# A gather-bound expert stage: the first head's routing split in two halves of eight rows, with the dot operand's scaling between them

## The chip, the cores and the metric

The kernel runs on one core of one Trainium2 chip. The metric is the device time of one execution in microseconds. Below, TensorE is PE, VectorE is DVE, ScalarE is ACT, GpSimd is POOL and SyncE is SP, as in the profile.

## What is computed

Two transformer-like blocks follow each other over 256 tokens of width 1024. The change touches only the second half of the first block, a mixture of experts whose rows are looked up by two-part keys:

```python
def _peer(h, w_q, sub_keys_1, sub_keys_2, expert_u, expert_v):
    q = (h @ w_q).reshape(B, S, PEER_HEADS, PEER_DKEY)
    s1 = jnp.einsum('bshd,nd->bshn', q[..., :half], sub_keys_1)
    s2 = jnp.einsum('bshd,nd->bshn', q[..., half:], sub_keys_2)
    v1, i1 = lax.top_k(s1, PEER_TOPK)
    v2, i2 = lax.top_k(s2, PEER_TOPK)
    cand = (v1[..., :, None] + v2[..., None, :]).reshape(..., PEER_TOPK * PEER_TOPK)
    best, ci = lax.top_k(cand, PEER_TOPK)
    expert_idx = i1[ci // PEER_TOPK] * PEER_NKEYS + i2[ci % PEER_TOPK]
    gates = jax.nn.softmax(best, axis=-1)
    ...
    a = jax.nn.gelu(einsum('td,thkd->thk', hx, u)) * gx
    return einsum('thk,thkd->td', a, v)
```

There are 8 heads, 128 keys on each side, 16 rows chosen for each token and head, and `h` is the normed, scaled and shifted residual (`h2` in the code). A row of the table `experts` holds `u` and `v` of one expert, 2048 float32 numbers or 8 KB.

## The kernel before

All five engines run hand-written instruction streams that are tied together by semaphores; nothing reorders them. 256 tokens are two tiles of 128, so there are 16 "heads" of work: eight for the first tile of tokens, eight for the second.

**Queries and scores.** PE multiplies the residual by the query weights in 16 blocks, `query(b)` (lines 1114 to 1149 order them), each as three passes (lines 770 to 772: the high part of the operands with the high part, and each low part with the other's high part). The weights come in eight chunks, `pq` 0 to 7, two blocks each. For a chunk ACT writes the high part (`part`, line 1346, semaphore `w_hi`) and DVE the low part (`rest`, line 1959, semaphore `w_lo`), and PE waits for `w_lo` before the first product of a block. `head_scores(h)` multiplies two blocks by the keys; DVE's `scores(h, t)` scales the result into `s_all` and counts up the semaphore `scores`.

**The operand of the dots.** DVE scales the residual by the norm (line 2425, semaphore `n2_scaled`), ACT adds the shift (`shift_h2`, line 1599, semaphore `h2`), PE transposes it in four steps (`turn_h2(0..3)`, line 1080; the third waits for four counts of `scores`, because it writes into banks that the scores of head 1 were in), and ACT copies it to `h2tok` (line 1620).

**Routing.** For a head DVE picks the top 16 keys on each side, adds them into 256 candidates, picks the best 16 and turns them into row numbers `rowid`. `route(h, even)` does it in one go (lines 2321 to 2361, then `name_rows`, whose line 2304 counts up `rows_ready`). It is used for heads 0 and 1; later heads have the same work spread between their dots.

**Gathers, dots, values.** POOL's `first_rows` (lines 684 to 703) issues indirect DMAs (line 659), one for each row slot: 128 expert rows, 1 MB. It waits for `rows_ready` 1, issues slots 0, 1, 4, 5 of head 0; waits for `query(5)` and issues slots 2, 3, 6, 7; waits for `rows_ready` 2 and issues slots 0, 1 of head 1 (`pair(1, 1, 0)`, into the memory of head 0's slots 0, 1, so after their use), then slots 2, 3 of head 1 (`pair(1, 1, 1)`, which waits until `values(1)` has used head 0's slots 2, 3), then slots 8, 9 of head 0, and so on. The slots 0 to 7 share a home with the next head's, and all wait for `v_used`, which PE counts up. DVE's `dot` (line 2377) multiplies two slots with `h2tok`, ACT's `weigh` (lines 1604 to 1615) makes diagonal matrices of the results, and PE's `values(p)` (line 1109) adds the weighted second halves.

**The order on DVE around the change** is the code at lines 2418 to 2456: scores of head 0, `route(0, 0)`, the scaling, `both_scores(1)`, `rest()`, the softmax weights, the first pair of dots, `route(1, 1)`, the second pair. The `rest()` there makes the low part of chunk `pq` 4, which is for PE's `query(8)` and `query(9)`. Those stand on PE after `values(0)` and `head_scores(3)` and before `values(1)` and `values(2)`. On ACT, `soften(0)` (line 1562, the exponentials of head 0) waits for the semaphore `best` and stands ahead of `shift_h2`.

Of the kernel before, what the change touches and what calls it, by code (L numbers as in the profile page):

```python
# [17 lines left out]
ALU = mybir.AluOpType  # L18
ACT = mybir.ActivationFunctionType
X = mybir.AxisListType.X  # L20

P = 128
# [3 lines left out]
KD = D // P  # L26
# [12 lines left out]
TAKEN = -3e38  # L39
# [183 lines left out]
def two_blocks(nc, w, out):  # L223
    with ExitStack() as ctx:
# [1078 lines left out]
        def _(act):  # L1303
# [254 lines left out]
            def soften(g):  # L1558

                act.wait_ge(S("best"), g + 1)  # L1560
                act.sem_inc(S("tick"), 1)
                act.activation(expb, best, ACT.Exp, bias=gst[:, 0:1], accum_out=gst[:, 1:2]).then_inc(S("best_exp"), 1)
# [19 lines left out]
            def copy_shifted(h):  # L1582


                act.wait_ge(S("score_mm"), 2 * h + 1)
                if h >= 2:
                    act.wait_ge(S("scores"), NT * (h - 1))
                at = h % 2 * 2 * NKEY
                act.activation(shifted[:, at:at + 2 * NKEY], BK[3][:, at:at + 2 * NKEY], ACT.Copy).then_inc(S("shifted"), 1)
# [3 lines left out]
            act.wait_ge(S("norm_ss"), norm_count("n2"))  # L1593
            inverse_root(stat[:, 1, :], BK[5][:, 0:T], D, "n2_root")

            def shift_h2():
                for k in range(KD):
                    act.wait_ge(S("n2_scaled"), k + 1)
                    act.activation(hT[:, k, :], hT[:, k, :], ACT.Identity, bias=adaT[:, 24 + k:25 + k]).then_inc(S("h2"), 1)

# [31 lines left out]
            part()  # L1632
            take_query(4)
            copy_shifted(1)
            soften(0)
            shift_h2()
            take_query(5)
            for i in range(4):
                copy_h2(i)
# [267 lines left out]
        def _(v):  # L1907
# [398 lines left out]
            def route(h, even):  # L2306
# [54 lines left out]
                v.sem_inc(S("head_step"), -n[0])  # L2361
                name_rows(even)

            def soft_weights(g, even):

                v.wait_ge(S("best_exp"), g + 1)
                v.sem_inc(S("tick"), 1)

                def body(step):
                    step(v.reciprocal(gst[:, 2:3], gst[:, 1:2]))  # L2370
                    step(v.tensor_scalar(soft[:, even, :], expb, gst[:, 2:3], None, ALU.mult))
                by(body)
# [45 lines left out]
            v.wait_ge(S("n2_root"), 1)  # L2418
            link(v.reciprocal(csil[:, 0:2], csil[:, 2:4]))
            scores(0, 0)  # L2420
            route(0, 0)
            scores(0, 1)
            v.wait_ge(S("n2_root"), 2)
            for k in range(KD):
                stt(hT[:, k, :], xT[:, k, :], mod[:, k:k + 1], stat[:, 1, :]).then_inc(S("n2_scaled"), 1)
            both_scores(1)
            rest()
            soft_weights(0, 0)
            v.wait_ge(S("h2tok"), 2)
            dot(0, 0, 0, 0)  # L2430
            route(1, 1)
            dot(0, 0, 0, 1)
            both_scores(2)
            dot(0, 0, 0, 2)
# [420 lines left out]
```

## Time and profile before

| | us |
|---|---|
| median of 3 runs | 1351.63 (1350.41 to 1352.51) |
| the profiled execution's own time | 1353.7 |
| its span | 1352.0 |
| PE busy | 1215.2 (90%) |
| DVE busy | 1059.7 (78%) |
| ACT busy | 616.0 (46%) |
| POOL busy | 290.1 (21%) |
| DMA of the gathers (queue 0) | 268.45 MB of 416.64 MB |

The page gives busy time for each engine, a picture of the span in 40 slices of 33.8 us (the digits are tenths of busy time; GB/s is what the DMA engines moved), and groups of instructions. Busy PE isn't PE at its peak, and the share of the whole span says little here: the stage of the change runs from about 307 us to 360 us, and the gathers behind it go on to about 950 us. So the rows below are read from the timeline and from stretches of it.

### The profile page before, as it was taken

The numbers are of one execution on the slowest core, as the hardware profiler recorded it, in microseconds if no ns is written. First come the engines' busy times: TensorE is split into PE (matmuls) and PEld (weight loads), VectorE is DVE, ScalarE is ACT, GpSimd is POOL, SyncE is SP. The second block draws the span as 40 slices with busy tenths as digits, with TensorE's granted clock in tenths as the row PEclk, the third lists the DMA queues.
The fourth block names the chain that finished last, engine by engine and source line by source line (L and its number), as shares of the span: only waits on it lengthen the run. The fifth ranks groups of instructions, "written<-read, shape, count | busy, mean of one in ns | idle before, by whom it ended". The sixth has DMA issues, their size and how long they took to land. (4 is left out here: it accounts for less than half of the span.)

```text
span 1352.0 us, 19494 instructions
## 1 busy us (share of the span) xinstructions
PE 1215.2 (90%) x6952; PEld 908.0 (67%) x6952; DVE 1059.7 (78%) x2161; ACT 616.0 (46%) x1265; POOL 290.1 (21%) x280
## 2 busy tenths in 40 slices
PE   7999999999989877778877777787899999999998
PEld 5999999999743333324332232333699999999998
DVE  7898678887879777777766777777699978898666
ACT  4666555656333333332433333233563265554445
POOL 1010000002545544344444434443000000000000
PEclk9999999999999999999999999999999999999999
DMA  9966446665999999999999999999853545454461
GB/s 388 384 225 249 187 158 235 245 234 234 375 422 426 427 428 428 427 427 427 427 427 427 427 428 428 428 427 428 341 187 126 187 137 183 180 187 173 174 236 43
DMA packets 55488, 416.64 MB, mean 308 GB/s; under 512 B 6113, under 2 KB 6753, under 8 KB 9202
## 3 DMA queue, kind: packets, MB, share of 16 engines
q0 software_dynamic: 37152, 268.45, 47.2%
q1 hardware_dynamic: 17792, 146.51, 29.3%
q8 instruction: 50, 0.82, 0.2%
q10 hardware_dynamic: 466, 0.63, 0.1%
q14 instruction: 28, 0.23, 0.0%
HBM read 414.52 MB, written 1.05 MB: 307 GB/s over the span
## 5 line engine op out<-in xcount | busy, mean ns | idle before, releaser
L1109 PE MATMUL ps<-arena 128*128 128x512 f32 x512 | 234.6, 603 | 57.0 <-ACT arena L1613 57.0
L1109 PE MATMUL ps<-ring,arena 128*128 128x512 f32 x440 | 214.1, 637 | 47.1 <-ACT arena L1613 47.1
L2377 DVE CUSTOM_DVE_ANT_0 arena<-arena 128x1024 f32<-128x1024 f32 x128 | 151.7, 1223 | 99.0 <-DMA arena<-in_experts,rowid 96.3
L1109 PEld LDWEIGHTS ps<-arena 128*128 128x128 f32 x512 | 92.7, 189 | 193.9 <-ACT arena L1613 98.0
L659 POOL DMA_INDIRECT arena<-in_experts,rowid x128 | 128.7, 1005 | 351.7 <-DVE rowid L2304 191.0
L1109 PEld LDWEIGHTS ps<-ring,arena 128*128 128x128 f32 x440 | 86.1, 202 | 170.4 <-issue 92.6
L772 PE MATMUL ps<-h_hi,w_lo 128*128 128x256 f32 x700 | 194.9, 278 | 0.0
L1606 ACT ACTIVATE arena<-arena 128x2 f32<-128x2 f32 x126 | 25.6, 203 | 369.1 <-DVE arena L2377 368.9
L770 PE MATMUL ps<-h_hi,w_hi 128*128 128x256 f32 x672 | 189.0, 281 | 3.0 <-DVE w_lo L1959 2.4
L771 PE MATMUL ps<-h_lo,w_hi 128*128 128x256 f32 x672 | 187.2, 279 | 0.0
L2377 DVE CUSTOM_DVE_ANT_0 ring<-ring,arena 128x1024 f32<-128x1024 f32 x112 | 133.3, 1222 | 35.4 <-DMA ring<-in_experts,rowid 26.5
L659 POOL DMA_INDIRECT ring<-in_experts,rowid x110 | 127.1, 1155 | 133.2 <-PE ps L1109 98.9
L1959 DVE TENSOR_TENSOR w_lo<-arena,w_hi 128x4096 fp32r<-128x4096 f32 (+1 forms) x30 | 122.1, 4069 | 29.7 <-ACT w_hi L1346 29.1
L1346 ACT ACTIVATE w_hi<-arena 128x4096 fp32r<-128x4096 f32 (+1 forms) x30 | 100.4, 3346 | 76.2 <-DMA arena<-in_up_w 32.1
L772 PEld LDWEIGHTS ps<-h_hi,w_lo 128*128 128x128 f32 x700 | 132.3, 189 | 0.0
L770 PEld LDWEIGHTS ps<-h_hi,w_hi 128*128 128x128 f32 x672 | 127.3, 190 | 4.1 <-DVE w_lo L1959 3.0
L771 PEld LDWEIGHTS ps<-h_lo,w_hi 128*128 128x128 f32 x672 | 127.1, 189 | 0.2
L770 PE MATMUL ps<-n_hi,e_hi 128*128 128x256 f32 (+1 forms) x352 | 101.4, 288 | 0.2 <-issue 0.2
L771 PE MATMUL ps<-n_lo,e_hi 128*128 128x256 f32 (+1 forms) x352 | 98.1, 279 | 0.0
L772 PE MATMUL ps<-n_hi,e_lo 128*128 128x256 f32 (+1 forms) x352 | 98.1, 279 | 0.0
L1959 DVE TENSOR_TENSOR e_lo<-ring,e_hi 128x2048 fp32r<-128x2048 f32 (+1 forms) x38 | 86.3, 2271 | 11.4 <-ACT e_hi L1346 10.8
L1613 ACT ACTIVATE arena<-ident,arena 128x128 f32<-128x128 f32 x252 | 85.4, 386 | 0.0
(424 smaller groups left out, 2558.4 us busy)
## 6 DMA issues: line engine op xcount, KB each, us to landing
ring<-in_early_w SPq DMA_DIRECT2D x43, 1024.0 KB, 5.0
arena<-in_ada_w SPq DMA_DIRECT2D x24, 1024.0 KB, 8.1
arena<-in_up_w SPq DMA_DIRECT2D x11, 2048.0 KB, 7.8
arena<-in_z_w SPq DMA_DIRECT2D x8, 2048.0 KB, 7.9
arena<-in_down_w SPq DMA_DIRECT2D x8, 1408.0 KB, 6.1
arena<-in_o_w SPq DMA_DIRECT2D x2, 2048.0 KB, 8.1
arena<-in_early_w SPq DMA_DIRECT2D x3, 1024.0 KB, 7.6
arena<-in_experts,rowid POOLq DMA_INDIRECT x128
```

The lines of the kernel that those rows point to most:

```text
L659: pool.indirect_dma_start(out=rows[j], out_offset=None, in_=w["experts"], in_offset=bass.IndirectOffsetOnAxis(ap=rowid[:, even, j:j + 1], ...
L770: pe.matmul(out, hi[:, k, c0:c0 + m], x_hi[:, k, :], start=k == 0, stop=False, skip_group_check=True)
L771: pe.matmul(out, hi[:, k, c0:c0 + m], x_lo[:, k, :], start=False, stop=False, skip_group_check=True)
L772: return pe.matmul(out, lo[:, k, c0:c0 + m], x_hi[:, k, :], start=False, stop=k == KD - 1, skip_group_check=True)
L1109: mm = pe.matmul(BK[4 + 2 * t + b], diag[:, j, :], rows[j][:, D + b * 512:D + (b + 1) * 512], start=first and j == 0, stop=last and j == ( ...
L1346: act.activation(hi, whole, ACT.Copy).then_inc(S("w_hi"), 1)
L1606: act.activation(gel[:, even, two], dots[:, even, two], ACT.Gelu).then_inc(S("act_head"), 1)
L1613: act.activation(diag[:, j, :], ident[:, :], ACT.Copy, scale=amul[:, even, j:j + 1]).then_inc(S("diag"), 1)
L1959: v.tensor_tensor(lo, whole, hi.bitcast(F32), ALU.subtract).then_inc(S("w_lo"), 1)
L2377: v.tensor_tensor_reduce(out=u, in0=u, in1=h2tok[:, t, :], scale=1.0, scalar=0.0, op0=ALU.mult, op1=ALU.add, accum_out=dots[:, even, j:j + ...
```

## The change

The first head's routing, `route(0, 0)`, becomes three pieces. `route_first` does the top keys of both sides, the candidates and the best eight with their positions. `name_eight(slice(0, 8))` turns these eight into row numbers and counts up `rows_ready`. After the scores of the second tile and the scaling of the dot operand, `route_second` picks the other eight (and counts up `best`), and `name_eight(slice(8, 16))` names them. The `rest()` for chunk `pq` 4 goes from ahead of the softmax weights to behind `route(1, 1)`. On ACT, `shift_h2` is cut in two: four of its eight instructions now stand ahead of `soften(0)`. `soft_weights` here is unchanged.

```diff
@@ ACT
-            def shift_h2():
-                for k in range(KD):
+            def shift_h2(ks):
+                for k in ks:
...
             take_query(4)
             copy_shifted(1)
+            shift_h2(range(4))
             soften(0)
-            shift_h2()
+            shift_h2(range(4, KD))
             take_query(5)
@@ DVE
+            def route_first():
...
+                for i in range(2):
+                    found = mark(v.max_index(topu[:, i, 8:16], top[:, i, 8:16], more[i]))
+                after(sums)
+                high = mark(v.max(best[:, 0:8], cand.rearrange("p a b -> p (a b)")))
+                after(found)
+                v.tensor_copy(topi[:, :, :], topu[:, :, :])
+                after(high)
+                after(mark(v.max_index(ciu[:, 0, 0:8], best[:, 0:8], cand.rearrange("p a b -> p (a b)"))))
+                v.sem_inc(S("head_step"), -n[0])
+
+            def name_eight(js):
...
+                def body(step):
+                    v.tensor_scalar(ciu[:, 1, js], ciu[:, 0, js], 4, None, ALU.logical_shift_right)
+                    step(v.tensor_scalar(ciu[:, 2, js], ciu[:, 0, js], EK - 1, None, ALU.bitwise_and))
+                    step(v.tensor_copy(ci[:, :, js], ciu[:, 1:3, js]))
+                    step(v.tensor_tensor(
+                        found, iota16[:, :].rearrange("p (c b a) -> p c b a", c=1, b=1).broadcast_to([P, 2, 8, EK]),
+                        ci[:, :, js].rearrange("p c (a b) -> p c a b", b=1).broadcast_to([P, 2, 8, EK]), ALU.is_equal))
+                    step(v.tensor_tensor(
+                        found, found, topi[:, :, :].rearrange("p c (b a) -> p c b a", b=1).broadcast_to([P, 2, 8, EK]),
+                        ALU.mult))
+                    step(v.tensor_reduce(pick[:, :, js], found, X, ALU.add))
+                    step(stt(pick[:, 0, js], pick[:, 0, js], float(NKEY), pick[:, 1, js], ALU.mult, ALU.add))
+                by(body)
+                return v.tensor_copy(rowid[:, 0, js], pick[:, 0, js])
+
+            def route_second():
...
+                def body(step):
+                    step(v.match_replace(cf2, best[:, 0:8], cf, TAKEN))
+                    step(v.max(best[:, 8:16], cf2))
+                    v.tensor_scalar(gst[:, 0:1], best[:, 0:1], -1.0, None, ALU.mult).then_inc(S("best"), 1)
+                    step(v.max_index(ciu[:, 0, 8:16], best[:, 8:16], cf2))
+                by(body)
...
             scores(0, 0)
-            route(0, 0)
+            route_first()
+            name_eight(slice(0, 8)).then_inc(S("rows_ready"), 1)
             scores(0, 1)
             v.wait_ge(S("n2_root"), 2)
             for k in range(KD):
                 stt(hT[:, k, :], xT[:, k, :], mod[:, k:k + 1], stat[:, 1, :]).then_inc(S("n2_scaled"), 1)
+            route_second()
+            name_eight(slice(8, EK))
             both_scores(1)
-            rest()
             soft_weights(0, 0)
             v.wait_ge(S("h2tok"), 2)
             dot(0, 0, 0, 0)
             route(1, 1)
+            rest()
             dot(0, 0, 0, 1)
```

On DVE, the first head from its ninth to sixteenth best on. Before, from the search for the second eight to the scaling:

```order
L2350 MAX_INDEX ciu<-arena 128x8
L2351 TENSOR_SCALAR ciu<-ciu 128x16
L2352 TENSOR_SCALAR ciu<-ciu 128x16
L2353 CAST arena<-ciu 128x32
L2354 TENSOR_TENSOR arena<-iota,arena 128x512
L2357 TENSOR_TENSOR arena<-arena 128x512
L2360 TENSOR_REDUCE arena<-arena 128x32
L1917 SCALAR_TENSOR_TENSOR arena<-arena 128x16
L2304 CAST rowid<-arena 128x16
L1917 SCALAR_TENSOR_TENSOR arena<-ps,csil,arena 128x256
L1917 SCALAR_TENSOR_TENSOR h_rows<-xT,mod,stat 128x256 x8
```

The same place on DVE in the changed kernel, from the search for the first eight's positions on:

```order
L2401 MAX_INDEX ciu<-arena 128x8
L2409 TENSOR_SCALAR ciu<-ciu 128x8
L2410 TENSOR_SCALAR ciu<-ciu 128x8
L2411 CAST arena<-ciu 128x2x8
L2412 TENSOR_TENSOR arena<-iota,arena 128x256
L2415 TENSOR_TENSOR arena<-arena 128x256
L2418 TENSOR_REDUCE arena<-arena 128x2x8
L1918 SCALAR_TENSOR_TENSOR arena<-arena 128x8
L2421 CAST rowid<-arena 128x8
L1918 SCALAR_TENSOR_TENSOR arena<-ps,csil,arena 128x256
L1918 SCALAR_TENSOR_TENSOR h_rows<-xT,mod,stat 128x256 x8
L2428 MATCH_REPLACE arena<-arena 128x256
```

The three wide instructions that name the rows have half the elements, and the second eight is picked only after the scaling; its naming repeats rows L2409 to L2421 once more, and only then come the scores of head 1.

On DVE, around the routing of head 1, whose last instruction writes `rowid`. Before, from its last wide instruction to the scores of head 2:

```order
L2360 TENSOR_REDUCE arena<-arena 128x32
L1917 SCALAR_TENSOR_TENSOR arena<-arena 128x16
L2304 CAST rowid<-arena 128x16
L2377 ISA arena<-arena 128x1024
L2377 ISA arena 128x1
L1917 SCALAR_TENSOR_TENSOR arena<-ps,csil,arena 128x256 x2
```

After:

```order
L2361 TENSOR_REDUCE arena<-arena 128x32
L1918 SCALAR_TENSOR_TENSOR arena<-arena 128x16
L2305 CAST rowid<-arena 128x16
L1960 TENSOR_TENSOR pq_ring<-ring,pq_ring 128x2048
L2447 ISA arena<-arena 128x1024
L2447 ISA arena 128x1
L1918 SCALAR_TENSOR_TENSOR arena<-ps,csil,arena 128x256 x2
```

The low part of chunk `pq` 4 now stands between the routing of head 1 and the second pair of dots (a pair is two such ISA instructions with a read of the sum behind each). On PE and POOL no instruction moves.

## Rows read from the trace of the kernel before

**Rows 1.** The page, part 2: what the DMA engines moved, in 40 slices.
```profile
GB/s 388 384 225 249 187 158 235 245 234 234 375 422 426 427 428 428 427 427 427 427 427 427 427 428 428 428 427 428 341 187 126 187 137 183 180 187 173 174 236 43
```

**Rows 2.** Stretches: length, engines' busy time (instructions), PEclk, DMA share, GB/s.
```profile
308.00:316.00 8.00, 8.00 (x66) 7.90 (x66) 7.79 (x34) 6.54 (x8) 0.00 (x0) 1.00 0.00 0
320.00:344.00 24.00, 23.32 (x166) 20.23 (x165) 19.36 (x55) 12.34 (x29) 8.52 (x8) 1.00 1.01 423
344.00:350.00 6.00, 6.00 (x20) 2.96 (x19) 5.75 (x10) 3.07 (x6) 2.70 (x3) 1.00 0.73 264
350.00:360.00 10.00, 10.00 (x66) 8.09 (x65) 9.22 (x24) 5.00 (x11) 7.89 (x5) 1.00 0.98 351
360.00:940.00 580.00, 466.17 (x1115) 199.02 (x1114) 432.83 (x1116) 200.42 (x670) 256.38 (x242) 0.97 1.01 427
```

**Rows 3.** Timeline of POOL: start, length, operation, idle before and its releaser.
```profile
316.99 1.09 POOL L659 DMA_INDIRECT arena<-in_experts,rowid  x1 [181.67 <-DVE rowid L2304]
...
323.12 1.37 POOL L659 DMA_INDIRECT arena<-in_experts,rowid  x1 [1.03 <-PE ps L772]
...
338.12 0.94 POOL L659 DMA_INDIRECT arena<-in_experts,rowid  x1 [9.29 <-DVE rowid L2304]
...
346.69 0.94 POOL L659 DMA_INDIRECT arena<-in_experts,rowid  x1 [6.33 <-PE ps L1109]
...
349.90 3.05 POOL L659 DMA_INDIRECT h_rows<-in_experts,rowid  x1 [0.30 <-issue]
...
357.87 2.97 POOL L659 DMA_INDIRECT arena<-in_experts,rowid  x1 [1.19 <-issue]
```

**Rows 4.** Timeline of PE around turn_h2, query(6), head_scores(3), query(8), values(1).
```profile
321.89 1.91 PE L1080 MATMUL ps<-ident,h_rows 128*128 128x128 f32 x16
323.55 0.36 PE L770 MATMUL ps<-x_hi,pq_ring 128*128 128x258 f32 x1
...
334.24 0.61 PE L1066 MATMUL ps<-keyT,arena 128*128 128x128 f32 x4
...
335.50 0.36 PE L770 MATMUL ps<-x_hi,pq_ring 128*128 128x258 f32 x1
...
342.18 0.70 PE L1109 MATMUL ps<-arena 128*128 128x512 f32 x1 [0.68 <-ACT arena L1613]
```

**Rows 5.** Timeline of DVE: routing of head 0, rest, dots, routing of head 1.
```profile
312.11 0.42 DVE L2345 FIND_INDEX8 ciu<-arena 128x8 uint32<-128x256 f32 x1
...
312.97 0.42 DVE L2350 FIND_INDEX8 ciu<-arena 128x8 uint32<-128x256 f32 x1
...
313.92 0.69 DVE L2354 TENSOR_TENSOR arena<-iota,arena 128x512 f32<-128x512 f32 x1
...
316.53 0.17 DVE L2304 CAST rowid<-arena 128x16 uint32<-128x16 f32 x1
...
321.38 2.29 DVE L1959 TENSOR_TENSOR pq_ring<-ring,pq_ring 128x2048 fp32r<-128x2048 f32 x1
...
326.79 1.23 DVE L2377 CUSTOM_DVE_ANT_0 arena<-arena 128x1024 f32<-128x1024 f32 x1 [2.77 <-DMA arena<-in_experts,rowid]
...
337.11 0.17 DVE L2304 CAST rowid<-arena 128x16 uint32<-128x16 f32 x1
```

**Rows 6.** Timeline of DVE, later: the same naming steps on 256 elements.
```profile
380.92 0.42 DVE L2295 TENSOR_TENSOR arena<-arena 128x256 f32<-128x256 f32 x1
381.38 0.42 DVE L2298 TENSOR_REDUCE arena<-arena 128x16 f32<-128x256 f32 x1
```

**Rows 7.** Timeline of DVE: two later low parts, beside two gathers of rows 3.
```profile
349.85 2.28 DVE L1959 TENSOR_TENSOR pq_ring<-ring,pq_ring 128x2048 fp32r<-128x2048 f32 x1
...
357.74 2.29 DVE L1959 TENSOR_TENSOR pq_ring<-ring,pq_ring 128x2048 fp32r<-128x2048 f32 x1
```

**Rows 8.** Timeline of ACT: the shifts of the dot operand; the last diagonals before values(1).
```profile
318.87 3.31 ACT L1599 ACTIVATE h_rows<-h_rows,adaT 128x256 f32<-128x256 f32 x8
...
341.45 0.68 ACT L1613 ACTIVATE arena<-ident,arena 128x128 f32<-128x128 f32 x2
```

More of the change, by code:

```diff
@@ L2362, in route, with mark, after @@
                 name_rows(even)
+            def route_first():
+                n = [0]
+                def mark(ins):
+                    n[0] += 1
+                    ins.then_inc(S("head_step"), 1)
+                    return n[0]
+                def after(at):
+                    v.wait_ge(S("head_step"), at)
+                keys = [s_all[:, 0, i * NKEY:(i + 1) * NKEY] for i in range(2)]
+                more = [cur2[:, i * NKEY:(i + 1) * NKEY] for i in range(2)]
+                first = [mark(v.max(top[:, i, 0:8], keys[i])) for i in range(2)]
+                left = []
+                for i in range(2):
+                    after(first[i])
+                    left.append(mark(v.match_replace(more[i], top[:, i, 0:8], keys[i], TAKEN)))
+                second = []
+                for i in range(2):
+                    after(left[i])
+                    second.append(mark(v.max(top[:, i, 8:16], more[i])))
+                for i in range(2):
+                    v.max_index(topu[:, i, 0:8], top[:, i, 0:8], keys[i])
+                after(second[1])
+                sums = mark(v.tensor_tensor(cand, top[:, 0, :].rearrange("p (a b) -> p a b", b=1).broadcast_to([P, EK, EK]),
+                                            top[:, 1, :].rearrange("p (b a) -> p b a", b=1).broadcast_to([P, EK, EK]),
+                                            ALU.add))
+                for i in range(2):
+                    found = mark(v.max_index(topu[:, i, 8:16], top[:, i, 8:16], more[i]))
[6 more added lines that the diff above has]
+                v.sem_inc(S("head_step"), -n[0])
@@ new lines, in name_eight @@
+            def name_eight(js):
+                found = oneh.rearrange("p a b -> p (a b)").rearrange("p (c a b) -> p c a b", c=2, b=EK)
+                def body(step):
[12 more added lines that the diff above has]
+                return v.tensor_copy(rowid[:, 0, js], pick[:, 0, js])
@@ new lines, in route_second @@
+            def route_second():
+                cf, cf2 = cand.rearrange("p a b -> p (a b)"), cand2.rearrange("p a b -> p (a b)")
+                def body(step):
[4 more added lines that the diff above has]
+                by(body)
```

## The prediction

> **What bounds the kernel now.** I read the 40 slices first. From about 372 us to 946 us the DMA engines move 422 to 428 GB/s in every slice [rows 1]: that is the ceiling this kernel reaches, so the long middle of the kernel is bound by the gathers' bytes. Then I cut the part ahead of it into stretches [rows 2]. From 308 to 316 us nothing is moved; from 320 to 344 us the engines are full (423 GB/s); from 344 to 360 us they are not (264, then 351 GB/s); from 360 to 940 us they are full again at 427 GB/s. So the time at which the gathers end is the time at which the last hole closes, near 360 us, plus bytes that the change doesn't alter. Lost in the hole, against 427 GB/s: 6 x (1 - 264/427) + 10 x (1 - 351/427) = 2.3 + 1.8 = 4.1 us. An earlier first gather is worth something only if this hole doesn't grow by as much.
>
> What opens the hole is on POOL's timeline [rows 3]: after the pair at 338.12 us POOL stands idle for 6.33 us until PE (line 1109, values(1)) releases it at 346.69 us. And PE isn't waiting for gathers there: it is busy for 23.3 of the 24 us from 320 to 344 us [rows 2], with one gap of 0.68 us ahead of values(1) at 342.18 us, which ended with the diagonals that ACT began at 341.45 us [rows 4, 8]. So the hole is closed by PE's chain turn_h2, query(6), query(7), values(0), head_scores(3), query(8), query(9), values(1), then POOL's issues.
>
> **The earlier start.** Before, the first eight's positions are found by 312.11 + 0.42 = 312.53 us with a replace of 0.5 us ahead of that search, the wide steps take 0.69 us each, and rowid is written by 316.53 + 0.17 = 316.70 us [rows 5]. The new chain leaves out the replace (about 0.4 us), the second max and the second search (0.86 us: from 312.53 us to that search's end at 312.97 + 0.42 = 313.39 us [rows 5]), and runs three wide steps at 0.42 instead of 0.69 us [rows 5, 6], 0.81 us together. That is 0.4 + 0.86 + 0.81 = 2.07 us, and I take 2.05 us: rowid's first eight at 314.65 us, POOL's first issue at 314.94 instead of 316.99 us. POOL's next four wait for query(5) at 323.12 us [rows 3], the same as before, since PE is untouched up to there. The first four gathers are 4.2 MB, 9.8 us at 427 GB/s, so the engines stay fed until then.
>
> **The later second half, on DVE.** What was left out comes back after the scaling: replace, max and search (0.4 + 0.86 us and the waits between them, about 1.5 us) and a second naming (313.39 to 316.70 us before, 3.3 us, less the 0.81 us: about 2.45 us). The scaling itself starts 2.05 us earlier. So head 1's scores end at 321.34 - 2.05 + 1.5 + 2.45 = 323.2 us instead of just before 321.38 us [rows 5]: 1.9 us late. PE's third turn_h2 waits for them. The 16 transposes run from 321.89 to 323.55 us, so the third group is due at 321.89 + 8 x 0.104 = 322.7 us [rows 4]. PE stalls for about 0.6 us, and query(6) starts at 324.15 us. The halved shift on ACT costs nothing: eight shifts take 3.31 us from 318.87 us [rows 8]; four now go first, soften(0) (its `best` counts up near 319.4 us) takes its place at about 320.3 us, and the last shift ends near 322.2 us as before.
>
> **The moved low part.** This is the costly edit. The first pair of dots waited for its rows at 326.79 us [rows 5]; with the gathers 2.05 us earlier it starts at 324.75 us (DVE is free at 323.7 us, h2tok is there near 324.3 us). Dots and route(1, 1) take 10.5 us as before (326.79 to 337.28 us [rows 5]), so head 1's rows are named at 335.25 instead of 337.28 us. Only then comes the low part of chunk pq 4, 2.29 us [rows 5]: ready at 337.5 us, where it used to be ready at 323.67 us. query(8) needs it. PE started query(8) at 335.50 us [rows 4] and, with the 0.6 us above, would be there at 336.1 us. So it stalls for another 1.4 us and starts 2.0 us late. Before values(1) 0.68 us of that, and the time for the weights' load, is given back, because PE was waiting there: query(8) and query(9) took 5.85 us, so values(1) starts at 337.5 + 5.85 = 343.35 instead of 342.18 us [rows 4]. Its diagonals are no later: the second pair of dots ends near 339.9 us, ACT takes query(8) at 340.7 us and has the diagonals by 342.4 us. So POOL is released at 346.69 + 1.17 = 347.86 us [rows 3].
>
> **The sum.** The gathers' queue, 2.05 us ahead, now also runs dry 2.05 us earlier (near 344.7 us), and that gain is spent in the hole. What counts is how much later the hole closes: at most the 1.17 us of PE's chain. Part of that is returned by POOL itself. Its two longest issues, 3.05 us at 349.90 us and 2.97 us at 357.87 us (0.94 us is usual) [rows 3], stand beside DVE's low parts at 349.85 and 357.74 us [rows 7], and both end 0.8 us after them. The low part of 349.85 us comes about 0.75 us earlier now, since DVE leads there; that of 357.74 us comes 0.35 us later, as the scores of head 4 must come from PE first (due at 354.75 instead of 354.41 us). So the issue that is released at 357.87 + 1.17 = 359.04 us should end at 361.2 instead of 360.84 us: 0.35 us late. Between 0.35 and 1.17 us, I take 0.8 us. The rest of the kernel behind the gathers is shifted, not changed. Against the profiled execution: 1353.7 + 0.8 = 1354.5 us. That execution lies 2.1 us above the median of the runs, so the forecast for the median is 1351.63 + 0.8 = 1352.4 us.
>
> On these long issues the Trainium skill, "SBUF — State Buffer", section "Who interferes with whom", says that a VectorE instruction with two inputs in SBUF keeps GpSimd from reading through a port that both share, and that the one that comes second waits for all of the first. By that, moving a two-input low part to 335.2 us puts it on top of POOL's issues for head 1 (due at 336.07 us) and holds the first of them to about 338.3 us, so that this pair gains nothing over its 338.12 us. The rows 3 and 7 agree with the rule (3.05 us beside 2.28 us). It would not change the sum, if the queue still holds work until 339.8 us, but it takes the reserve away; the rival with the larger hole below is what it leads to if it doesn't.
>
> **Rivals.** (a) *The gain comes through.* If the hole is not set by PE's release but by how much has been gathered before, the whole earlier start counts: 1351.63 - 2.05 = 1349.6 us. For it: between 350 and 360 us the engines are busy (0.98) while moving only 351 GB/s [rows 2], so something other than a missing issue slows them there. Against it: POOL's idle 6.33 us before 346.69 us [rows 3], with a queue that ends just then. Chance 0.17. (b) *The hole grows on both sides and slows the rest, slower than before.* The queue is dry from 344.7 us until the issue of 347.86 us takes effect. If the DMA engines come back slower from an empty queue than from one nearly empty, or if values(3), 1.17 us late, opens a second hole before 359.04 us, the hole costs another 1 to 2.5 us: 1351.63 + 1.2 + 1 to 2.5 = 1353.8 to 1355.3 us. It decides as soon as what is queued at 347.86 us and behind doesn't last until 360 us. Chance 0.15. (c) *PE's stall doesn't happen as computed*, since the first dots start earlier than the landing suggests or query(8) meets its low part in time; then start and hole cancel: 1351.6 us. Chance 0.13. (d) Something larger in either direction, 0.05 faster and 0.02 slower.
>
> **Numbers.** The forecast (1352.0 to 1352.8 us) has 0.48. Within 0.2%, which is 2.7 us and about what a measurement of this kernel can tell from no change, lie the forecast, (a), (c) and nearly two thirds of (b): together 0.87, rounded down. Faster by more than 0.2% 0.06, slower by more 0.07. The range takes in (a) with 0.3 us for the spread of the runs, and (b) up to 1354.3 us.
>
> **What would show it.** In the profile after: first gather near 314.9 us; head 1's scores ending near 323.2 us, and a gap of about 0.6 us in PE's transposes; rowid of head 1 near 335.2 us, the low part right behind it, and a PE gap of about 1.4 us ahead of query(8) at 337.5 us; no gap before values(1) at 343.4 us; POOL's release near 347.9 us; fewer GB/s from 344 to 350 us than 264. If PE shows no gap ahead of query(8), the argument is wrong; if the gaps are there and the time still falls by 2 us, the reading of the hole is.

## The result and the profile after

| | kernel before | changed kernel |
|---|---|---|
| median, first measurement (22 runs each) | 1351.60 us | 1354.15 us |
| lowest to highest | 1349.58 to 1356.58 | 1351.72 to 1363.47 |
| ratio, 95% interval | | 1.0034 (1.0022 to 1.0046) |
| the profiled execution's own time, its span | 1353.7, 1352.0 | 1352.29, 1350.6 |

The changed kernel is slower, where no measurable difference was forecast: the measured ratio is 1.0034, as is that of the means, while that of the medians is 1.0019 (2.55 us). The means lie further apart because 8 of the 22 executions of the changed kernel took over 1359 us and none of the kernel before did; without executions above 1356.4 us the medians are 1353.62 and 1351.57 us, 2.05 us apart. Two later measurements of the same pair, on other chips, gave 1.0016 (0.9998 to 1.0035) and 1.0016 (0.9999 to 1.0033), which by themselves don't exclude "no change". The profiled execution is one of the shorter ones of the changed kernel, and that of the kernel before one of its longer ones, so their spans alone would say the opposite. Both kernels have some executions about 6 us longer than the others; what is different in these is shown under e8.

First the stage that the prediction was about. These are the stretches of [rows 2] in the changed kernel:

```profile
320.00:344.00 24.00, 22.66 (x164) 19.91 (x164) 22.02 (x63) 12.60 (x32) 8.79 (x7) 1.00 1.01 417
344.00:350.00 6.00, 6.00 (x16) 2.66 (x14) 5.75 (x8) 3.90 (x10) 2.07 (x2) 1.00 0.19 82
350.00:360.00 10.00, 10.00 (x64) 8.00 (x63) 7.99 (x24) 3.96 (x7) 6.86 (x6) 1.00 0.96 369
360.00:940.00 580.00, 464.02 (x1122) 198.87 (x1121) 433.02 (x1116) 200.65 (x670) 255.04 (x242) 0.98 1.01 427
```

From 344 to 350 us only 82 GB/s are left of 264; behind it the rate is a little higher (369 instead of 351), and from 360 us on it is the same 427. Lost against 427 GB/s: 6 x (1 - 82/427) + 10 x (1 - 369/427) = 4.8 + 1.4 = 6.2 us, 2.1 us more than before. The gathers start 1.98 us earlier. So gain and loss cancel, as the prediction had it in kind. POOL's timeline, for [rows 3]:

```profile
315.01 1.09 POOL L659 DMA_INDIRECT arena<-in_experts,rowid  x1 [179.51 <-DVE rowid L2421]
...
335.93 2.17 POOL L659 DMA_INDIRECT arena<-in_experts,rowid  x1 [8.06 <-DVE rowid L2305]
338.40 1.98 POOL L659 DMA_INDIRECT arena<-in_experts,rowid  x1 [0.31 <-issue]
347.63 1.98 POOL L659 DMA_INDIRECT arena<-in_experts,rowid  x1 [7.24 <-PE ps L1109]
...
358.72 2.21 POOL L659 DMA_INDIRECT arena<-in_experts,rowid  x1 [1.93 <-PE ps L1109]
```

PE's, for [rows 4]; the gaps stand in brackets with what ended them:

```profile
323.38 1.09 PE L1080 MATMUL ps<-ident,h_rows 128*128 128x128 f32 x8 [0.37 <-DVE arena L1918]
324.23 0.37 PE L770 MATMUL ps<-x_hi,pq_ring 128*128 128x258 f32 x1
...
337.34 0.39 PE L770 MATMUL ps<-x_hi,pq_ring 128*128 128x258 f32 x1 [0.97 <-DVE pq_ring L1960]
...
343.22 1.02 PE L1109 MATMUL ps<-arena 128*128 128x512 f32 x2
```

and DVE's, for [rows 5]:

```profile
324.59 1.22 DVE L2447 CUSTOM_DVE_ANT_0 arena<-arena 128x1024 f32<-128x1024 f32 x1 [0.66 <-DMA arena<-in_experts,rowid]
...
334.92 0.17 DVE L2305 CAST rowid<-arena 128x16 uint32<-128x16 f32 x1
335.00 2.29 DVE L1960 TENSOR_TENSOR pq_ring<-ring,pq_ring 128x2048 fp32r<-128x2048 f32 x1
```

Every local step came within 0.5 us of its forecast. What the prediction had not looked at is the end of the gathers. Here is DVE over the last pairs of dots, kernel before:

```profile
948.08 1.23 DVE L2377 CUSTOM_DVE_ANT_0 h_rows<-h_rows,arena 128x1024 f32<-128x1024 f32 x1 [1.99 <-DMA ring<-in_experts,rowid]
...
953.01 1.23 DVE L2377 CUSTOM_DVE_ANT_0 ring<-ring,arena 128x1024 f32<-128x1024 f32 x1 [2.54 <-DMA ring<-in_experts,rowid]
...
957.90 1.23 DVE L2377 CUSTOM_DVE_ANT_0 ring<-ring,arena 128x1024 f32<-128x1024 f32 x1 [2.51 <-DMA ring<-in_experts,rowid]
```

and changed kernel:

```profile
947.73 1.23 DVE L2447 CUSTOM_DVE_ANT_0 h_rows<-h_rows,arena 128x1024 f32<-128x1024 f32 x1 [2.00 <-DMA ring<-in_experts,rowid]
...
953.61 1.22 DVE L2447 CUSTOM_DVE_ANT_0 ring<-ring,arena 128x1024 f32<-128x1024 f32 x1 [3.50 <-DMA ring<-in_experts,rowid]
...
958.51 1.23 DVE L2447 CUSTOM_DVE_ANT_0 ring<-ring,arena 128x1024 f32<-128x1024 f32 x1 [2.52 <-DMA ring<-in_experts,rowid]
```

At 947.7 us the changed kernel is 0.35 us ahead. Its next pair waits 3.50 us for rows instead of 2.54 us, and from there on it is 0.6 us behind. (Below, this is the late pair: 5.88 us behind the pair ahead of it instead of 4.93 us.) In the DMA records an instruction packet of 8192 bytes (queue 14) starts at 951.5 us in the changed kernel; in the kernel before it starts at 961.5 us, when the last rows are in. The change puts ten DVE instructions more into the program (nine of them in the trace, and a semaphore wait), so everything behind them stands ten places further on, and the fetch comes ten places earlier. Whether that is the cause is what the second round of experiments asked.

### The profile page after: what moved, and what is told of

It is laid out like the page before. It is cut to its first block and busy times, and to the rows that moved or that the text cites. A ratio compares the mean times of both kernels' runs of the same rounds, so it can differ in the third digit from the quotient of the medians.

```text
span 1350.6 us, 19503 instructions
## 1 busy us (share of the span) xinstructions
PE 1211.1 (90%) x6952; PEld 906.0 (67%) x6952; DVE 1060.8 (79%) x2169; ACT 616.8 (46%) x1265; POOL 289.0 (21%) x280
## 3 DMA queue, kind: packets, MB, share of 16 engines
HBM read 414.52 MB, written 1.05 MB: 308 GB/s over the span
## 5 line engine op out<-in xcount | busy, mean ns | idle before, releaser
L1109 PE MATMUL ps<-ring,arena 128*128 128x512 f32 x440 | 211.0, 629 | 50.1 <-ACT arena L1613 50.1
```

The lines of the kernel that those rows point to most:

```text
L1109: mm = pe.matmul(BK[4 + 2 * t + b], diag[:, j, :], rows[j][:, D + b * 512:D + (b + 1) * 512], start=first and j == 0, stop=last and j == ( ...
```

## Experiments

Each ran on one chip beside runs of the kernel before. Single executions reach the change's stage at up to 2.1 us different times (first search of the first head's routing at 308.14 to 310.21 us), so for comparisons I subtract that time: "T+" is measured from the first MAX8 of this routing (308.50 us in the kernel before, 308.60 us in the changed one). On that clock the 251st gather's first packet starts at T+635.33 before, and the pair of dots that starts at 957.90 us before is at T+649.40.

### Which part of the change costs what

**e1, the changed kernel again,** with no edit.

> The changed kernel as it is, once more, to see how its single runs lie. The 22 runs so far fall into two groups: 12 near 1353.4 us (before: 1351.6), two near 1355.9, eight from 1359.3 to 1363.5. Theory (two parts): the hole in the gathers' queue closes about 1 to 2 us later in every run, and in about one run of three something adds another 7 to 8 us; so again two groups, with the same places, also on this one chip. Rival (chips differ, not runs): all runs here lie in one group, within 2 us of each other.

Measured 1354.31 us, ratio 1.0016 (0.9998 to 1.0035). One of the 11 executions lay near 1360 us, not one in three; in the kernel before, on the same chip, 5 of 28 took more than 1357 us. So the long executions aren't the changed kernel's own. Gathers at T+635.13. The late pair is there again, at 953.24 us, 5.88 us behind the one ahead of it. And in this execution there was a dip of PE's granted clock from 957.8 us on. PE over the last weighted sums, kernel before, then e1:

```profile
956.86 7.13 PE L1109 MATMUL ps<-ring,arena 128*128 128x512 f32 x16 [1.22 <-ACT arena L1613]
```

```profile
957.09 8.83 PE L1109 MATMUL ps<-ring,arena 128*128 128x512 f32 x16 [2.18 <-ACT arena L1613]
```

The same 16 matmuls take 1.70 us more, and the gap ahead of them is 0.96 us longer. The stretch from 957 to 962 us shows the clock (the eighth value: busy times, then PEclk, DMA share, GB/s), before and e1:

```profile
957.00:962.00 5.00, 5.00 (x12) 2.24 (x13) 4.10 (x7) 2.29 (x8) 0.00 (x0) 1.00 0.47 160
```

```profile
957.00:962.00 5.00, 4.91 (x8) 2.13 (x9) 3.86 (x7) 2.11 (x9) 0.00 (x0) 0.66 0.40 147
```

A mean of 0.66 over 5 us is 3.4 us at half (1.2 GHz) and the rest at full clock (2.4 GHz), and 1.7 us of work are lost. They aren't made up later: e6 and e10 are one program, the first with such a dip at 956.3 us and the second with none behind 950 us, and they end at T+1043.05 and T+1041.25.

**e2, the low part back at its old place,** the rest of the change kept.

```diff
             both_scores(1)
+            rest()
             soft_weights(0, 0)
...
             route(1, 1)
-            rest()
             dot(0, 0, 0, 1)
```

> The changed kernel with the low part of chunk pq 4 back ahead of the softmax weights. Theory (PE's stall ahead of query(8) makes the hole, and the dry queue is what the slow runs start from): no gap ahead of query(8), first dots at about 326.0 us instead of 324.6, rows of head 1 named near 336.5 us, POOL released at 346.8 to 347.0 us instead of 347.6, median 1351.6 us (1351.0 to 1352.3) and no runs near 1360 us. Rival (the split of the routing itself, by its earlier gathers, puts the queue into the slow group): runs near 1360 us are as frequent as in the changed kernel, median above 1353 us.

Measured 1352.54 us, ratio 1.0001 (0.9986 to 1.0017), 1.8 us below e1 on the same chip. PE has no gap ahead of query(8), POOL is released earlier, and the hole is smaller:

```profile
346.15 0.94 POOL L659 DMA_INDIRECT arena<-in_experts,rowid  x1 [5.92 <-PE ps L1109]
```

```profile
344.00:350.00 6.00, 6.00 (x24) 3.37 (x23) 5.75 (x8) 3.34 (x7) 3.24 (x3) 1.00 0.62 208
```

208 GB/s from 344 to 350 us instead of 82; gathers at T+633.97, 1.2 to 1.5 us ahead of the changed kernel. So the moved low part is what turns the earlier start into nothing. The late pair of dots is still there (5.89 us). The expected end of the long executions didn't come: two of 12 took 1357.9 and 1358.4 us, so that the dry queue isn't what makes them.

**e3, the low part moved alone,** in the kernel before (`rest()` behind `route(1, 1)`, nothing split).

> The kernel before with only the low part of chunk pq 4 moved behind route(1, 1). Theory (PE's chain closes the hole): the low part is ready near 339.5 us, query(8) starts 4.0 us late, of which 0.7 to 0.9 us is given back ahead of values(1), POOL is released near 349.8 us instead of 346.7, median 1351.6 + 3.1 = 1354.7 us or more, and many runs near 1361 us if a dry queue starts the slow group. Rival (the hole is not set by PE): within 0.5 us of 1351.6 us.

Measured 1357.71 us, ratio 1.0058 (1.0041 to 1.0074). Without the earlier start the low part comes later still, and POOL is released 4.5 us later than before on the T+ clock (5.1 us by the rows):

```profile
351.82 2.70 POOL L659 DMA_INDIRECT arena<-in_experts,rowid  x1 [8.73 <-PE ps L1109]
```

```profile
350.00:360.00 10.00, 10.00 (x51) 6.89 (x50) 6.80 (x18) 4.83 (x12) 6.65 (x6) 1.00 0.47 160
```

Gathers at T+640.16, 4.8 us later. The cost of this edit therefore depends on the split: it is 4.8 us alone, and 1.8 us beside it (by the averages given in the last part). The last dots come at their usual pace here (4.90 us), and this kernel has no added instruction.

**e4, head 1's scores ahead of the second half,** on top of e2, to take away PE's stall in the transposes.

```diff
+            both_scores(1)
             route_second()
             name_eight(slice(8, EK))
-            both_scores(1)
             rest()
```

> As the kernel with the low part back, and head 1's scores ahead of the second half of head 0's routing, so that PE's transposes don't wait either. Theory (PE's stalls are all that costs): no gap in the transposes, PE as in the kernel before, POOL released at 346.7 us or up to 0.1 us earlier, median 1350.9 to 1351.6 us, no runs near 1360 us. Rival (the early first gathers are worth their 2.05 us once PE doesn't stall): 1349.6 us. Second rival (the early gathers bring the slow runs): some runs near 1360 us here too.

Measured 1354.76 us, ratio 1.0027 (1.0012 to 1.0043). The stall doesn't go but grows, with another releaser: PE now waits 1.05 us for ACT's shifts, since `soften(0)`, which waits for `best`, stands ahead of the second four of them.

```profile
323.68 1.53 PE L1080 MATMUL ps<-ident,h_rows 128*128 128x128 f32 x12 [1.05 <-ACT h_rows L1599]
```

Gathers at T+634.80; late pair and clock dip near 958 us both there. The theory expected 1350.9 to 1351.6 us and failed. The 0.37 us of stall were not worth an edit.

### The late pair: the fetch or the routing

**e5, the kernel before again,** with no edit, as a measure of the scatter.

> The kernel before, nothing changed, as a second profile and as a measure of how far two measurements of the same program lie apart. Theory 1 (what stands behind 945 us decides): the ratio is 1.000 within 0.0015, the start of the last gathers lies within 1 us of the first profile's 943.8 us, and where the span differs by more than 1 us from 1352.0 us, the difference arises behind 945 us, as a dip of the granted clock near 958 us (about 1.7 us) or a slower pace of the matmuls between 1160 and 1320 us (about 6 us). Rival: the gathers' stage itself varies by 2 us or more between executions, and the last gathers start as far apart as the spans.

Measured 1350.52 us beside 1350.91 us, ratio 0.9990 (0.9975 to 1.0005), gathers at T+635.47. So a ratio 0.001 away from 1 is what one program can show against itself. Its trace joins the first one's up to 1150 us and then ends 1.9 us earlier: the first had a clock dip at 1160.7 us and this one none.

**e6, the kernel before with ten DVE instructions more,** ahead of the loop over heads (near 390 us, where DVE waits for rows anyway); the routing is untouched.

```diff
             name_rows(0)
+            for _ in range(5):
+                v.sem_inc(S("head_step"), 1)
+                v.sem_inc(S("head_step"), -1)
             with v.Fori(1, EH - 1, 2) as g:
```

> The kernel before with ten semaphore additions on DVE (five times plus one, minus one) ahead of the first loop over heads, where DVE has slack. Nothing of the routing is changed, but DVE's later instructions stand ten places further on, as they do in the changed kernel. Theory 1 (the fetch of DVE's instructions): the 8192-byte packet of the instruction queue moves from 961.5 us to about 951.5 us, the sixth pair of dots of the last head comes 5.9 us behind the fifth instead of 4.9 us (near 954 us), and the time is 1 us above that of the kernel before (ratio 1.0007). Rival: the later sixth pair belongs to the changed routing, and here the interval stays at 4.9 us and the time at that of the kernel before, wherever the packet lies.

Measured 1352.66 us beside 1350.91 us, ratio 1.0010 (0.9998 to 1.0022). The instruction packet moved to 949.8 us, and the late pair is there:

```profile
946.33 1.23 DVE L2377 CUSTOM_DVE_ANT_0 h_rows<-h_rows,arena 128x1024 f32<-128x1024 f32 x1 [1.99 <-DMA ring<-in_experts,rowid]
...
952.21 1.23 DVE L2377 CUSTOM_DVE_ANT_0 ring<-ring,arena 128x1024 f32<-128x1024 f32 x1 [3.51 <-DMA ring<-in_experts,rowid]
```

5.88 us instead of 4.93 us, with the routing of the kernel before. A clock dip near 957 us came with it.

**e7, the changed kernel with sixty such instructions** (thirty ahead of each loop over heads), which move the fetch to among the gathers.

> The changed kernel with sixty semaphore additions on DVE, thirty ahead of each of the two loops over heads, so that the instruction packet of 951.5 us is fetched some 40 us earlier, among the gathers. Theory 1 (the fetch): the sixth pair of dots comes 4.9 us behind the fifth, as in the kernel before, and the time is 1 us below that of the changed kernel: 1353.3 us, ratio about 1.001 against the kernel before. Rival: the interval stays at 5.9 us. Should the additions (1 to 2 us at each place) hold up the dots of a head, the last gathers start up to 2 us later than 944.1 us, which neither of them forecasts.

Measured 1352.28 us, ratio 1.0014 (1.0000 to 1.0029). No packet between 936 and 968 us, and the pair is on time, with the changed routing:

```profile
947.82 1.23 DVE L2447 CUSTOM_DVE_ANT_0 h_rows<-h_rows,arena 128x1024 f32<-128x1024 f32 x1 [2.00 <-DMA ring<-in_experts,rowid]
...
952.74 1.23 DVE L2447 CUSTOM_DVE_ANT_0 ring<-ring,arena 128x1024 f32<-128x1024 f32 x1 [2.54 <-DMA ring<-in_experts,rowid]
```

So the late pair goes with the fetch and not with the routing: shown in both directions. The packets' records show how. The instruction packet takes 0.31 us, as long as one expert row, but the row packet that starts as it ends (951.83 us in the changed kernel) takes 0.84 us instead of 0.31 us. This is so in all seven traces with the fetch near 950 us, and in the others no row packet from 945 to 962 us takes over 0.4 us. The two make 0.84 of the 0.96 us. Among the gathers, from 400 to 945 us, a row packet of 0.5 to 0.85 us follows on every 8 KB instruction packet too (8 or 9 in each trace); there the rate from 360 to 940 us stays 427 GB/s. Why that row packet is long is not shown. Against the start of the 251st gather the pair behind the late one (957.90 us before) comes only 0.5 us later: 14.6 us behind it on average in the seven traces with the fetch near 950 us (14.44 to 14.99), 14.1 us in eight without (13.72 to 14.37; e12, with PE in another order, is left out). The rest of the 0.96 us is a lead that DVE had at 947 us and lost.

The Trainium skill, "Runtime: NRT & Kernel Launch", section "Instruction fetch mechanics", says that the sequencer fetches the next block through its own DMA queue while it executes the present one, and that crossing a block is mostly hidden. For DVE itself the traces agree: what ended its 3.50 us of waiting was the landing of rows. What isn't hidden is the effect on a transfer beside it, the row packet of 0.84 us.

**e8, both repairs:** e2's edit and the sixty instructions.

> The split routing with the low part of chunk pq 4 back at its old place, and the same sixty semaphore additions. With the low part back, the last gathers started at 942.3 us, 1.5 us ahead of the kernel before. Theory 1 (the start is worth 1.5 us and the fetch takes 1 us of it): sixth pair 4.9 us behind the fifth, time 1.5 us below the kernel before, 1350.1 us, ratio 0.9989. Rival (the gain of the gathers' stage is given back behind 960 us, by the phase of the clock dips or the pace of the late matmuls): the last gathers start near 942.3 us and the ratio is still 1.000 or above.

Measured 1350.57 us beside 1350.91 us, ratio 0.9996 (0.9983 to 1.0009); gathers at T+633.58, pair on time. The profiled execution, though, took 1358.25 us, and its trace shows where such an execution loses 6 us. The stretch from 1200 to 1260 us, dense query and feed-forward matmuls, kernel before and e8:

```profile
1200.00:1260.00 60.00, 60.00 (x532) 60.00 (x531) 54.34 (x82) 28.99 (x28) 0.00 (x0) 1.00 0.45 163
```

```profile
1200.00:1260.00 60.00, 60.00 (x512) 60.00 (x511) 52.62 (x81) 27.96 (x27) 0.00 (x0) 1.00 0.45 163
```

512 matmuls instead of 532 in the same 60 us, with a granted clock of 1.00 in both. Their starts are 117.9 ns apart instead of 113.0 ns, from about 1160 to 1330 us, while DVE's and ACT's instructions there last as long as ever (the same median within 0.01 us in every group). In the other traces the 117.9 ns appear as well, but only in stretches of 10 to 60 us, between 970 and 1150 us and near 1330 us. The long stretch was there in e2, e7 and e8 and in no other trace; e14 is the program of e7 and e11 that of e8, so it isn't the program's. The executions of 1359 to 1363 us in the first measurement are longer than these three, and none of them was traced.

### The same questions a second time

**e9, the kernel before with the sixty instructions.**

> The kernel before with sixty semaphore additions on DVE (thirty ahead of each loop, 2.8 us at each place by the 0.093 us that one took in the trace of the kernel with ten), so that its instruction packet is fetched among the gathers, not in the tail. Theory 1 (sixty additions cost nothing, as the gathers bound that stretch): last gathers start between 942.6 and 943.9 us as in three profiles of the routing before, sixth pair of dots 4.9 us behind the fifth, ratio 1.000. Then the ratio of the changed kernel with the same additions, 1.0014, is the cost of the changed routing without the fetch. Rival: the additions cost something themselves, and the ratio lies at 1.0005 to 1.001; then the changed routing is that much cheaper than 1.0014 says.

1351.40 us beside 1350.96 us, ratio 1.0007 (0.9999 to 1.0016); gathers at T+634.93, pair on time (4.92 us).

**e10, e6 again.**

> The same kernel as the first one with ten additions: a second profile and a second measurement of what the fetch at 950 us costs in all. Theory 1 (the fetch leaves PE idle ahead of 958 us, and that brings the clock dip near 958 us in many executions): sixth pair 5.9 us behind the fifth again, ratio 1.0007 to 1.0014 (1 to 1.9 us) against the kernel before, and with sixty additions in place of ten the ratio falls back to 1.000. Rival: the 1.75 us of the first measurement were chance, and ten and sixty additions give the same ratio.

1353.21 us, ratio 1.0017 (0.9998 to 1.0037): late pair (5.88 us), this time without a dip at 958 us. The medians with ten instructions thus lie 1.8 and 2.3 us above those beside them, with sixty 0.4 us. None of these intervals excludes 1.0000 by itself, so a cost of the fetch in time is likely but not shown.

**e11, e8 again.**

> The split routing with the low part at its old place and sixty additions, as run once before at a ratio of 0.9996. Theory 1 (the last gathers, 1.1 us ahead of the mean of three profiles of the routing before, are worth that much): ratio 0.9992, and in a profile without the slow matmuls of 1160 to 1320 us the span is 1.1 us below that of the kernel before. Rival (what is won at the gathers is lost again in the PE-bound tail): last gathers near 942.3 us again and a ratio of 0.9996 to 1.0005.

1351.58 us, ratio 1.0010 (0.9994 to 1.0027), gathers at T+633.18. Two measurements, 0.9996 and 1.0010: the 1.2 us by which its gathers lead don't show in the time, and no version that beats the kernel before was found. Nor was its theory (0.9992) met. On the T+ clock this execution ends at 1040.6 us, the kernels with the old routing and no dip behind 950 us (e5, e9, e10) at 1041.6, 1041.3 and 1041.3 us; that is a gain below what these measurements can hold.

**e12, the hole attacked directly:** on top of e8, PE's values(1) goes ahead of query(9), and ACT's diagonals for it ahead of taking query(8).

```diff
             query(8)
-            query(9)
             values(1)
+            query(9)
             values(2)
```

> The kernel of the run ahead of this with one more change: PE's values(1) stands between query(8) and query(9) instead of behind both, and ACT's diagonals for it ahead of taking query(8). This goes at the hole itself. Theory 1 (the hole is closed by PE's chain): the diagonals are there near 340.5 us, PE stands idle 1.3 us ahead of values(1), POOL is released near 344.8 instead of 346.2 us, but query(9) and all of PE behind it come 1.3 us later, so that a later release becomes late: last gathers within 0.7 us of 942.3 us, ratio 0.9996. Rival: bytes moved early count fully, the last gathers start 1.4 us earlier at 940.9 us, ratio 0.9986, which would beat both kernels. Third: PE's later releases decide, last gathers at 943.6 us, ratio 1.0003.

1356.68 us, ratio 1.0051 (1.0035 to 1.0067): all three theories were wrong. PE, from values(1) on:

```profile
341.24 5.40 PE L1109 MATMUL ps<-arena 128*128 128x512 f32 x8 [1.77 <-ACT arena L1613]
...
351.25 3.70 PE L1109 MATMUL ps<-arena 128*128 128x512 f32 x8 [1.73 <-ACT arena L1613]
```

PE starts values(1) 0.85 us earlier than e8, but the idle 1.77 us ahead of it is followed by a clock dip at 341.7 us, and the eight matmuls take 5.40 us where the next eight take 3.70 us. POOL is released at 347.44 us, later than in e2, and stands idle once more for 5.48 us ahead of its issue at 363.43 us. Gathers at T+638.02, 4.4 us later than e8. Moving a wait to where PE is otherwise busy cost the wait and the clock here; the idle 1.73 us ahead of 351.25 us, though, had no dip behind it.

### The changed kernel a third time

**e13, the changed kernel, and e14, it with the sixty instructions,** on one chip.

> The changed kernel as it is, a third time. Theory 1 (executions 6 us longer come by chance, at about one in six, in both kernels): 1 to 4 of some 12 executions above 1357 us, much as in the kernel before, the rest around 1352.5 to 1353.5 us, ratio 1.0015 to 1.0025; in the profile the last gathers start 635.3 us behind the first routing instruction of the first head and the sixth pair of dots 5.9 us behind the fifth. Rival (the change makes the slow pace frequent): 4 or more of 12, with 2 or fewer in 25 of the kernel before.

> The changed kernel with sixty semaphore additions, a second time. Theory 1: no fetch in the last dots, sixth pair 4.9 us behind the fifth, no clock dip near 958 us, ratio 1.0010 to 1.0015, and 1 to 1.5 us below the changed kernel without additions on the same chip. Rival: the two lie within 0.5 us of each other, and the fetch was not worth more than the 0.4 us by which the last dots come late.

e13: 1354.21 us, ratio 1.0016 (0.9999 to 1.0033); gathers at T+635.52, late pair (5.88 us), clock dip at 958.8 us. e14: 1353.19 us, ratio 1.0000 (0.9980 to 1.0019); gathers at T+635.60, pair on time (4.92 us), no dip. The median without the fetch is 1.0 us lower here, as expected, though the two intervals overlap. As to the long executions: above 1356.4 us lay 8 of 22 of the changed kernel and 1 of 22 of the kernel before in the first measurement, 2 of 11 and 5 of 28 in the second, 3 of 12 and 7 of 23 here. Together that is 13 of 45 and 13 of 73; on the two other chips the kernel before had 2 of 35 and 4 of 29. So the share differs from chip to chip, and the bound isn't sharp: e13's trace, at 1356.49 us, has two dips and no long slow stretch. That the change makes the slow matmuls more frequent is neither shown nor excluded.

**The dips.** In ten traces the granted clock dipped at 799 to 803 us and again 78.5 us later, at 877 to 881 us; one such step further is 956 to 960 us. Five of them have the fetch near 950 us, and four of these dipped near 958 us (e1, e4, e6, e13; not e10). Five don't have it (before, e8, e9, e11, e14), and none dipped there. This fits a dip that needs both the pattern, which differs from execution to execution, and the longer idle time of PE ahead of its last weighted sums (2.18 us in e1, 1.22 us before). The changed kernel's first trace and e2, whose pattern was another, had the fetch and no dip. Four of five against none of five is a hint and no proof; I didn't vary the idle time by itself.

## Why the prediction was wrong

- **The earlier start** (first issue 314.94 us, 2.05 us earlier): 315.01 us, right.
- **The later second half** (scores end 323.2 us, stall 0.6 us, query(6) 324.15 us): scores end at 323.3 us, stall 0.37 us, query(6) 324.23 us. Right.
- **The moved low part** (rowid of head 1 by 335.25 us, gap 1.4 us, query(8) 337.5 us): 335.1 us, 0.97 us, 337.34 us. The gap reads smaller since it counts from the modelled end of the last scores' matmul; from head_scores(3) to query(8) it took 337.34 - 334.87 = 2.47 us instead of 1.26 us [rows 4], so the delay is 1.2 us. Right, and e2, e8 and e11 show its worth: without it the gathers start at T+633.58 on average, 1.8 us ahead of the five traces with it.
- **values(1) and POOL's release** (343.35 and 347.86 us, no gap): 343.22 and 347.63 us. Right. Not foreseen: this issue starts just behind a dot (DVE at 347.57 us) and takes 1.98 instead of 0.94 us.
- **POOL's issues beside a low part** (the first for head 1 held to 338.3 us): it began at 335.93 us and took 2.17 us, to 338.10 us, where 0.94 us is usual. The long issues of [rows 3] became shorter (1.91 us at 349.91 us and 2.21 us at 358.72 us), and the low parts found others: 2.80 us at 323.43 us in e2, whose low part is made there. In the 16 traces 48 issues begin inside a low part, and every one ends 0.81 us behind it. The rule that the prediction took from the Trainium skill, "SBUF — State Buffer", section "Who interferes with whom", agrees with that. The late end at 361.2 us that was forecast came at 360.93 us, 0.1 instead of 0.35 us later than before.
- **The hole's close** (0.35 to 1.17 us later, 0.8 us taken): five traces with the changed routing (changed kernel, e1, e7, e13, e14) have the 251st gather at T+635.38 on average, and five with the old one (before, e5, e6, e9, e10) at T+634.82. That is 0.56 us, with a scatter of 0.6 us in a single trace. The difference is there near the 20th gather already (0.6 us). It agrees with the 0.8 us that was forecast, but the two traces of the kernel before itself (635.33 and 635.47) lie among those of the changed one (635.13 to 635.60), so its size is not sharply known. Rival (a) fell, but it is what happens as soon as the hole is not made worse: with the low part in place 1.2 us of the 2.05 us come through to the last gathers (634.82 against 633.58).
- **"The rest of the kernel behind the gathers is shifted, not changed"**: this step failed: it put at nothing, without a reason, what the edit could do there. The change adds ten instructions to DVE's program, and that moves a fetch from behind the last rows to among them. In the last dots it costs 0.5 us (0.96 us of PE's idle time), and in four of seven traces a clock dip of 1.7 us with it, about 1.0 us on average. Ten instructions without effect, put into the kernel before, move the same fetch, and its medians are 1.8 and 2.3 us higher (e6, e10; both intervals just include no change). By these estimates the sum is 0.6 + 0.5 + 1.0 = 2.1 us, against 2.55 us between the medians of the first measurement, and 2.2 and 1.0 us in the later two. The ends of the traces don't bear out its first two terms. Leave out e7 with its long slow stretch, take 1.7 us off for each dip behind 950 us and up to 1200 us, and the changed routing ends at T+1041.7 on average (changed kernel, e1, e13, e14; 1041.1 to 1042.4), the old one at T+1041.4 (before, e5, e6, e9, e10; 1041.3 to 1041.8). So what is seen in full is the dip, whose link with the fetch is a hint, and what the medians hold beyond it stays open; so does the larger part of the ratio of 1.0034, which is in the eight executions above 1359 us.
- **The size of "no difference"**: I gave 0.87 to it since the forecast, (a) and (c) lay inside 0.2%. With 0.8 us already spent, the margin to 2.7 us was 1.9 us, and nothing in the working said how well the 390 us behind the gathers were known. The 0.07 for slower came from one mechanism in the hole alone, and it was too small for that one as well: of rival (b)'s 1353.8 to 1355.3 us about one third lies within 2.7 us of 1351.63 us, not nearly two thirds, which makes 0.83 for "no difference" and some 0.12 for slower.

Rival (b) gave the right sum, 1353.8 to 1355.3 us, by the wrong mechanism: there was no second hole, and from 360 us on the engines moved 427 GB/s as before.

## What to carry to other kernels

An edit that adds or takes away instructions on an engine moves later instruction fetches of that engine; look in the trace of before for where its instruction packets fall relative to stretches in which something waits for a DMA, and test with instructions that do nothing whether a small difference is the edit's or the shift's. When a producer is to start earlier, look for who ends the next wait behind it: here it was PE's chain, which the same edit made longer, so that 2 us of head start were spent in the queue's next hole. And keep a bound of its own for what isn't traced through: a stage that is full of dense matmuls has no slack, and idle time ahead of it may cost the clock as well.

## What the runs showed of the hardware

- An 8 KB instruction packet near 950 us, in a stretch where every pair of dots waits for rows, makes one pair wait 3.50 instead of 2.54 us (seven traces), and none does with the packet elsewhere. The row packet right behind an 8 KB instruction packet takes up to 0.84 us instead of 0.31 us, here and among the gathers, in every trace.
- A gather's issue on POOL that begins inside DVE's 2.29 us low part ends 0.81 us behind it (48 issues in 16 traces); the 93 issues in the trace of before that begin while DVE does nothing take 0.93 to 0.95 us.
- The dips of the granted clock near 958 us last 3.4 us at half, and cost 1.70 us of dense matmuls (8.83 against 7.13 us). Near 340 us only two kernels had one, and both had PE idle just ahead of it: 1.77 us in e12 (dip at 341.7 us) and 3.77 us in e3 (dip at 340.0 us).
- Matmuls can run 4% slower (117.9 against 113.0 ns from start to start) for 170 us with the granted clock shown as 1.00. It comes and goes between executions of one program (e8 and e11, e7 and e14), and accounts for about 6 us in the three traces that have it. What sets it is open.
- The programs here are the same up to the first routing instruction, 308 us into the kernel, and executions reach it up to 2.1 us apart (two of one program, e8 and e11, 1.5 us); differences below that between two traces mean nothing unless they are taken from a common instruction.
